# A two-layer trunk on one core: the first norm's squares in token layout, the gates' products in other banks, and a rebuilt start

## The chip, the cores and the metric

One core of a Trainium2 chip runs the whole program. Its engines are TensorE (PE: matmuls; PEld: the loads of their weights), VectorE (DVE), ScalarE (ACT), GpSimd (POOL) and SyncE (SP, which here only issues DMAs). Each works through its own instructions in order and waits on semaphores for the others. The metric is the device time of one execution in microseconds, the lower the better.

## The reference

The input x has 1024 tokens of 1024 numbers (fp32). Two layers follow, each a token mixer and a squared-ReLU MLP with residuals: the mixer of layer 0 is an mLSTM with 4 heads, that of layer 1 differential attention. A last norm ends it. The change lies in the first norm and in the mLSTM's input products and gates:

```python
def rmsnorm(x, g):
    y = xf * lax.rsqrt(jnp.mean(xf * xf, axis=-1, keepdims=True) + EPS)
    return (y * g.astype(jnp.float32)).astype(x.dtype)
...
    q, k, v, o, ig, fg = jnp.split(u @ w_in, splits, axis=-1)      # u = rmsnorm(h, ln_mix[0])
    log_i = softcap(ig.astype(f32) + bg[:nh], GATE_SOFTCAP)
    log_f = jax.nn.log_sigmoid(softcap(fg.astype(f32) + bg[nh:], GATE_SOFTCAP))
...
    b = jnp.cumsum(lf, axis=-1)                                    # inside each chunk of 128 tokens
    m_new = jnp.maximum(bl + m_st, ml)                             # from chunk to chunk, 8 chunks
...
    h = h + mix
    h = h + sq_relu_mlp(rmsnorm(h, ln_mlp[i]), w_up[i], w_down[i])
```

## The kernel before, in words

Activations are kept transposed: `h` has 128 channels on the partitions, 8 channel tiles `d`, and 1024 tokens along the free axis in two halves of 512. Products are made in three parts from split numbers (`hi` times `hi`, weight `lo` times `hi`, weight `hi` times `lo`), 128x512 each, so one panel of 128 output channels takes 2 halves x 8 tiles x 3 = 48 products (L1183 to L1185). The norm is applied after the product: a product leaves PSUM through `take` (L2465, VectorE), which multiplies it by `rstd_bc`, the reciprocal root of the mean square of each token, spread over all partitions.

The order on every engine is the order in which the code is written, apart from semaphores. The start, before:

- SyncE loads x in 8 pieces (`x_tok`, tokens on the partitions), then the gates' bias and `lam`, then panels of weights.
- For each of 8 channel tiles TensorE transposes 8 blocks of x into `aps` (L1446). VectorE copies the first half of the tokens to `h` (L2821), ScalarE the second (L2091). ScalarE rounds `h` times the norm's gain to `one_hi` (L2094), VectorE makes the rest, `one_lo` (L2406). ScalarE squares `h` (L2101), VectorE adds the squares of two tiles (L2816), and TensorE sums them over channels with 8 products by a column of ones (L1433, into `mps`), four times.
- The gate products (36 columns in two parts, L1462, L1463, L1466) follow their tile by two steps, into `dps`.
- `norm(0)` makes `rstd` on VectorE (L2442 and the chain behind it), TensorE spreads it (L1222, inside the first half of the first panel), VectorE copies it to `rstd_bc` (L2446).

Then come six panels, called panel 0 to 5 here. Each has two halves that take turns in the two `dps` banks; a half may start when the half before the last has been taken (`evac`). GpSimd splits the weights of a panel into hi and lo (L909, L914) and between two splits subtracts activation blocks (L1069) that ScalarE scales first (L2109) and rounds after (L2119). Beside the panels ScalarE and VectorE work out the gates: tanh, exp and log (L2146 to L2151), running sums (L2945), a running maximum over 8 chunks (L2955, L2959) with two subtractions for each chunk (L2962, L2968), exponentials (L2160 to L2164), then the selection of rows. TensorE joins in with 8 transposes (`gate_transposes`, L1478) and 4 products that spread one head's rows (`broadcast_rows`, L1487). VectorE reads these (`take_rows`, L2982, L2986) and splits the first weights of the next stage (`mix_low`, L2865). That stage, the mixer's products for the other heads (`mix_steps`, from L1506), starts behind panel 5. Its first product waits for the `take` of panel 5's first half and for `mix_low(0)`. Its first product is called the mix start here.

## Time and profile before

| | |
|---|---|
| three runs | 2242.74, 2242.92, 2241.22 us (median 2242.74) |
| profiled execution, first to last instruction | 2241.5 us (1.2 us under the median; what lies outside the span isn't listed by itself) |
| TensorE busy | 2209.4 us, 99% |
| TensorE weight loads | 1836.1 us, 82% |
| VectorE, ScalarE, GpSimd busy | 1640.5, 973.7, 873.3 us (73%, 43%, 39%) |
| first product of panel 0 | at 38.35 us |
| mix start | at 108.98 us |

A busy share is a mean over the whole span. Matmuls overlap, so a row of 390 ns with the next row 227 ns behind it stands for 227 ns of TensorE's time. The granted clock (PEclk) is a share of full speed.

### The profile page before, as it was taken

Reading aid. Unit: us, or ns where it says so; the run is one execution under the profiler, and the core shown is the slowest. Engines: PE = TensorE matmul, PEld = TensorE weight load, DVE = VectorE, ACT = ScalarE, POOL = GpSimd, SP = SyncE. Lnnn points to the kernel's source line nnn. Section 1 sums busy time; section 2 is a strip of 40 time slices with the busy share of each in tenths; the row PEclk is TensorE's granted clock in tenths of the full one; section 3 lists DMA queues with packets and bytes.
Section 4 is the critical chain, followed back from the end, with each engine's and each line's share of the span. In section 5 each row is a group of like instructions: output and inputs, shape, how many; then the busy total and the mean of one; then the engine's idle time right before and its main releaser. Section 6 shows DMA issues by size and latency. Waiting matters only on the chain.

```text
span 2241.5 us, 28700 instructions
## 1 busy us (share of the span) xinstructions
PE 2209.4 (99%) x10501; PEld 1836.1 (82%) x10501; DVE 1640.5 (73%) x2141; ACT 973.7 (43%) x1613; POOL 873.3 (39%) x805
## 2 busy tenths in 40 slices
PE   8999999999999999999999999999999999999998
PEld 6888887888888888888888888877888888888887
DVE  6867766499659479399577777786599569388397
ACT  6354444244343343345244455564354243343346
POOL 4845546200234233230766666675200234232320
PEclk9999999999999999999999999999999999999999
DMA  8677743363551632701522222222463542633601
GB/s 256 222 269 253 242 150 98 124 262 118 188 188 38 248 128 98 272 25 36 162 67 66 66 66 66 66 76 76 159 226 113 196 179 71 248 113 123 234 0 76
DMA packets 139844, 317.37 MB, mean 142 GB/s; under 512 B 8609, under 2 KB 82514, under 8 KB 126546
## 3 DMA queue, kind: packets, MB, share of 16 engines
q1 hardware_dynamic: 137552, 315.78, 41.1%
q8 instruction: 73, 1.20, 0.2%
q10 hardware_dynamic: 2178, 0.06, 0.1%
q14 instruction: 41, 0.34, 0.0%
HBM read 242.41 MB, written 56.62 MB: 133 GB/s over the span
## 4 chain that ended last, share of the span: by engine, by line
PE 92%; DVE 4%; ACT 2%; issue 1%; DMA 0%; POOL 0%; ACTq 0%; DVEq 0%; POOLq 0%
PE aps L1317 10%; PE aps L1321 10%; PE aps L1319 10%; PE mps L1317 4%; PE mps L1321 4%; PE dps L1317 4%; PE dps L1321 4%; PE mps L1319 4%; PE dps L1319 4%; PE dps L1183 3%; PE dps L1185 3%; PE dps L1184 3%; PE dps L1201 3%; PE dps L1203 3%; PE dps L1202 3%; PE mps L1677 2%
## 5 line engine op out<-in xcount | busy, mean ns | idle before, releaser
L1317 PE MATMUL aps<-b_ring,w_hi 128*128 128x512 f32 x640 | 249.3, 390 | 0.0
L1321 PE MATMUL aps<-b_ring,w_hi 128*128 128x512 f32 x640 | 249.0, 389 | 0.0
L1319 PE MATMUL aps<-b_ring,w_lo 128*128 128x512 f32 x640 | 249.0, 389 | 0.0
L1031 POOL TENSOR_TENSOR s_blk<-s_blk,a 128x1024 f32<-128x1024 f32 x24 | 68.6, 2859 | 379.4 <-DVE w_lo L2521 253.1
L2539 DVE TENSOR_TENSOR b_ring<-h,b_ring 128x1024 fp32r<-128x1024 f32 x120 | 206.3, 1726 | 5.6 <-ACT b_ring L1915 5.6
L909 POOL TENSOR_TENSOR w_hi<-w_raw,ones 128x256 fp32r<-128x256 f32 (+1 forms) x133 | 121.9, 946 | 201.7 <-PE dps L1203 103.8
L1023 POOL TENSOR_TENSOR s_blk<-a,a22u 128x1024 f32<-128x1024 f32 x12 | 34.9, 2907 | 327.0 <-DMA a<-in_w_up 320.0
L1317 PE MATMUL aps<-b_ring,a_hi 128*128 128x512 f32 x384 | 149.8, 390 | 0.0
L1321 PE MATMUL aps<-b_ring,a_hi 128*128 128x512 f32 x384 | 149.4, 389 | 0.0
L1319 PE MATMUL aps<-b_ring,a_lo 128*128 128x512 f32 x384 | 149.4, 389 | 0.0
L1317 PEld LDWEIGHTS aps<-b_ring,w_hi 128*128 128x128 f32 x640 | 120.1, 188 | 25.4 <-issue 0.7
L1319 PEld LDWEIGHTS aps<-b_ring,w_lo 128*128 128x128 f32 x640 | 120.1, 188 | 25.0
L1321 PEld LDWEIGHTS aps<-b_ring,w_hi 128*128 128x128 f32 x640 | 120.1, 188 | 25.0
L1915 ACT ACTIVATE b_ring<-h 128x1024 fp32r<-128x1024 f32 x112 | 116.5, 1048 | 49.8 <-DVE h L2574 35.1
L1201 PE MATMUL dps<-one_hi,w_hi 128*128 128x512 f32 x320 | 136.6, 427 | 0.0
L1879 ACT ACTIVATE w_hi<-s_blk 128x1024 fp32r<-128x1024 f32 x68 | 71.9, 1058 | 135.1 <-PE aps L1321 92.0
L1943 ACT ACTIVATE h<-h 128x1024 f32<-128x1024 f32 x64 | 67.8, 1060 | 140.6 <-DVE h L2643 132.3
L2521 DVE TENSOR_TENSOR w_lo<-s_blk,w_hi 128x1024 fp32r<-128x1024 f32 x68 | 87.7, 1289 | 53.3 <-ACT w_hi L1879 53.3
L1203 PE MATMUL dps<-one_lo,w_hi 128*128 128x512 f32 x320 | 126.0, 394 | 0.0
L1202 PE MATMUL dps<-one_hi,w_lo 128*128 128x512 f32 x320 | 125.5, 392 | 0.0
L2328 ACT ACTIVATE at<-mps 128x384 f32<-128x384 f32 (+2 forms) x120 | 46.9, 425 | 158.0 <-PE mps L1670 157.7
L914 POOL TENSOR_TENSOR w_lo<-w_raw,w_hi 128x256 fp32r<-128x256 f32 (+1 forms) x133 | 112.3, 873 | 2.9
(514 smaller groups left out, 6363.0 us busy)
## 6 DMA issues: line engine op xcount, KB each, us to landing
b_ring<-xs SPq DMA_DIRECT2D x42, 2048.0 KB, 7.9
xs<-b_ring SPq DMA_DIRECT2D x14, 2048.0 KB, 7.8
one_hi<-xm SPq DMA_DIRECT2D x19, 1024.0 KB, 5.0
one_lo<-xm SPq DMA_DIRECT2D x19, 1024.0 KB, 7.5
a<-in_w_up SPq DMA_DIRECT2D x16, 1024.0 KB, 5.4
a<-in_w_down SPq DMA_DIRECT2D x16, 1024.0 KB, 7.9
w_raw<-in_diff_w_in SPq DMA_DIRECT2D x24, 512.0 KB, 4.0
mix_a<-in_mlstm_w_in SPq DMA_DIRECT2D x36, 256.0 KB, 7.4
```

Of the source, the lines that this page charges most:

```text
L909: last = nc.gpsimd.tensor_tensor(hi[:, cut], w_raw[:, slot, cut], ones[:, :].unsqueeze(1).broadcast_to([P, piece, P]), ALU.mult)
L914: last = nc.gpsimd.tensor_tensor(lo[:, cut], w_raw[:, slot, cut], hi[:, cut].bitcast(f32), ALU.subtract)
L1201: nc.tensor.matmul(dps[:, half], w_hi[:, slot, k], rh, start=(k == 0), stop=False)
L1202: nc.tensor.matmul(dps[:, half], w_lo[:, slot, k], rh, start=False, stop=False)
L1203: last = nc.tensor.matmul(dps[:, half], w_hi[:, slot, k], rl, start=False, stop=(k == NT - 1))
L1317: nc.tensor.matmul(to[:, n], wh, ring[:, 0, k], start=new and k == 0, stop=False, skip_group_check=not new)
L1319: nc.tensor.matmul(to[:, n], wl, ring[:, 0, k], start=False, stop=False, skip_group_check=not new)
L1321: last = nc.tensor.matmul(to[:, n], wh, ring[:, 1, k], start=False, stop=(k == 3), skip_group_check=not new)
L1879: nc.scalar.activation(kt_view(A_HI[a % 3]), half_of(RAW[name], q), ACT.Copy).then_inc(a_hi, 1)
L1915: last = nc.scalar.activation(to, tiles_of(src, q), ACT.Copy)
L2521: nc.vector.tensor_tensor(kt_view(A_LO[a % 3]), half_of(RAW[name], q), kt_view(A_HI[a % 3]).bitcast(f32), ALU.subtract).then_inc(a_ready, 1)
L2539: last = nc.vector.tensor_tensor(lo, tiles_of(src, q), hi, ALU.subtract)
```

## The change

1. `sum_pair`, `add_squares` and the squares of `h` go: no squares in the loop over tiles. Behind the loop ScalarE squares `x_tok` in its own layout, 8 instructions of 128x1024 that also add up along the free axis (`accum_out`), which gives the sum of each token. `first_norm` makes `rstd` from it; it is spread after the first tile of panel 1.
2. The gate products go to `mps` and follow their tile by three steps; VectorE makes `one_lo` of tile 0 before it splits the gates' weights.
3. TensorE starts with 8 products of `ones` by `ones` into `dps`, which nothing reads.
4. Panel 0's high part is made by ScalarE behind tile 5; GpSimd makes only the low part.
5. Panel 0 goes to `dps`, panel 1 to `aps` banks 2 and 3, panel 2 to `dps`: the first two panels wait for no `take`. `gate_transposes` moves into panel 5 (it was in panel 4), and `broadcast_rows` from between panels 4 and 5 to behind panel 5.
6. On VectorE small constant work moves ahead of the norm; the 16 subtractions of the gates become two over all chunks. SyncE issues the bias and `lam` behind the first two panels' weights.

```diff
-            split(1, 1, 1, first=True, piece=PIECE)
+            low_part(1, 1, panel0_hi, 1)
@@ TensorE @@
-            def half_panel(g, slot, half, hi, lo, ready=None, base=0, hooks={}, order=range(NT), taken=None, weights=None):
+            def half_panel(g, slot, half, hi, lo, ready=None, base=0, hooks={}, order=range(NT), taken=None, weights=None,
+                           to=None):
+                to = dps[:, half] if to is None else to
...
-                pe.wait_ge(evac, 2 * g + half - 1 if taken is None else taken)
+                if taken != 0:
+                    pe.wait_ge(evac, 2 * g + half - 1 if taken is None else taken)
...
-            def sum_pair(p):
-                pe.wait_ge(sq_added, p + 1)
-                for j in range(NB):
-                    last = nc.tensor.matmul(mps[:, 0, j:j + 1], squares_of(2 * p)[:, j // 4, (j % 4) * P:(j % 4 + 1) * P],
-                                            ones[:, 0:1], start=first, stop=True, skip_group_check=not first)
...
+            pe.wait_ge(pool_chain, 4)
+            for n in range(8):
+                nc.tensor.matmul(dps[:, 0, 0:P], ones[:, :], ones[:, :], start=True, stop=True)
             pe.wait_ge(const_ok, 4)
-            for s in range(NT + 2):
+            for s in range(NT + GATE_LAG):
...
-                    if s % 2 == 1:
-                        sum_pair((s - 3) // 2)
-
-            half_panel(G_MIX[0], G_MIX[0] % 2, 0, *one, hooks={3: lambda: broadcast_rstd(0)})
-            half_panel(G_MIX[0], G_MIX[0] % 2, 1, *one)
+            g = G_MIX[0]
+            for half in range(2):
+                half_panel(g, g % 2, half, *one, taken=0)
+            for half in range(2):
+                half_panel(g + 1, (g + 1) % 2, half, *one, taken=0, to=aps[:, 2 + half],
+                           hooks={0: lambda: broadcast_rstd(0)} if half == 0 else {})
+            for half in range(2):
+                half_panel(g + 2, g % 2, half, *one, taken=3 + half)
...
-            panels(G_MIX[0], G_MIX[0] % 2, 4, *one, skip=1)
-            half_panel(G_MIX[0] + 4, (G_MIX[0] + 4) % 2, 0, *one)
+            panels(G_MIX[0], G_MIX[0] % 2, 5, *one, skip=3)
+            half_panel(G_MIX[0] + 5, (G_MIX[0] + 5) % 2, 0, *one)
             gate_transposes()
-            half_panel(G_MIX[0] + 4, (G_MIX[0] + 4) % 2, 1, *one)
+            half_panel(G_MIX[0] + 5, (G_MIX[0] + 5) % 2, 1, *one)
             pe.wait_ge(gates_ready, 1)
             broadcast_rows(0)
-            panels(G_MIX[0], G_MIX[0] % 2, 6, *one, skip=5)
@@ ScalarE, in the loop over tiles and behind it @@
-                for half in range(2):
-                    last = nc.scalar.activation(squares_of(d)[:, half], h[:, d, cuts[half]], ACT.Square)
-                last.then_inc(sq_ready, 1)
+                if d == 5:
+                    act.wait_ge(w_ld[1], 16)
+                    nc.scalar.activation(w_hi[:, 1], w_raw[:, 1], ACT.Copy).then_inc(panel0_hi, 1)
...
+            for n in range(NB):
+                last = nc.scalar.activation(x_tok[:, n], x_tok[:, n], ACT.Square, accum_out=small[:, 4, n:n + 1])
+            last.then_inc(ss_done, 1)
@@ VectorE @@
-            def add_squares(p):
-                dve.wait_ge(sq_ready, 2 * p + 2)
-                to = squares_of(2 * p)
-                nc.vector.tensor_tensor(to[:, :, :], to[:, :, :], sq[:, :, :], ALU.add).then_inc(sq_added, 1)
...
-            mlstm_takes(0, 0, 16)
+            mlstm_takes(0, 0, 32)
...
-            mlstm_takes(0, 16, 24)
+            mlstm_takes(0, 32, 40)
             for c in range(NB):
-                if c == 4:
-                    mlstm_takes(0, 32, 40)
...
-                if c == 5:
+                if c == 3:
                     mlstm_takes(0, 40, 48)
-                nc.vector.tensor_scalar(g_astate[:, chunk[c]], g_m[:, chunk[c]], mst[:, c:c + 1], None,
-                                        ALU.subtract)
...
+            nc.vector.tensor_tensor(by_chunk[0], by_chunk[1], mst[:, 0:NB].unsqueeze(2).broadcast_to([MH, NB, P]),
+                                    ALU.subtract)
+            nc.vector.tensor_tensor(by_chunk[2], by_chunk[3], by_chunk[1][:, :, P - 1:P].broadcast_to([MH, NB, P]),
+                                    ALU.subtract)
+            mlstm_takes(0, 48, 56)
```

`mlstm_takes(0, a, b)` takes the halves between a/8 and b/8: 0 and 1 are panel 0's, 2 and 3 panel 1's, and so on.

On VectorE a piece of the loop over tiles, before (the third and the fourth tile, with the add of squares between them):

```order
L2821 COPY h<-aps 128x512 [waits xt_done]
L2406 SCALAR_TENSOR_TENSOR one_lo<-h,gains,one_hi 128x512 [waits emit_hi] x2
L2816 TENSOR_TENSOR relu<-relu,sq 128x1024 [waits sq_ready]
L2821 COPY h<-aps 128x512 [waits xt_done]
L2406 SCALAR_TENSOR_TENSOR one_lo<-h,gains,one_hi 128x512 [waits emit_hi] x2
```

The same engine, now, from the second tile's copy on:

```order
L2822 COPY h<-aps 128x512 [waits xt_done]
L2407 SCALAR_TENSOR_TENSOR one_lo<-h,gains,one_hi 128x512 [waits emit_hi,gain_ready]
L2407 SCALAR_TENSOR_TENSOR one_lo<-h,gains,one_hi 128x512 [waits emit_hi]
L2834 CAST w_hi<-w_raw 128x8x64 [waits gate_ld]
L2835 TENSOR_TENSOR w_hi<-w_raw,w_hi 128x8x36 [waits dve_chain]
L2822 COPY h<-aps 128x512 [waits xt_done]
L2407 SCALAR_TENSOR_TENSOR one_lo<-h,gains,one_hi 128x512 [waits emit_hi] x2
L2822 COPY h<-aps 128x512 [waits xt_done]
```

The four adds of 128x1024 are gone, and the gates' weights are split one step later, behind tile 0's low part.

On TensorE the end of the panels, before (L1478 the gates' transposes, L1487 the spread rows, L1506 the mix start):

```order
L1478 MATMUL aps<-ident,mo 128x128 x7
L1183 MATMUL dps<-one_hi,w_hi 128x512 [waits evac]
...
L1487 MATMUL aps<-rows_hl,sel 128x512 [waits sel_ready,gates_ready]
L1487 MATMUL aps<-rows_hl,sel 128x512 x3
L1183 MATMUL dps<-one_hi,w_hi 128x512 [waits evac,w_split]
...
L1506 MATMUL dps<-one_hi,w_hi 128x512 [waits evac,mx_lo]
```

The same place now:

```order
L1478 MATMUL aps<-ident,mo 128x128 x7
L1184 MATMUL dps<-one_hi,w_hi 128x512 [waits evac]
...
L1487 MATMUL aps<-rows_hl,sel 128x512 [waits sel_ready,gates_ready]
L1487 MATMUL aps<-rows_hl,sel 128x512 x3
L1506 MATMUL dps<-one_hi,w_hi 128x512 [waits evac,mx_lo]
```

The panel that stood between the spread rows and the mix start has moved ahead of them. On VectorE the order around this place is as it was; the reader of the spread rows and the next stage's first splits, now:

```order
L2998 COPY cols<-aps 128x32 [waits gt_done]
L2998 COPY cols<-aps 128x32 x2
L3001 MEMSET small 128x1 [waits dve_chain]
L2472 SCALAR_TENSOR_TENSOR mo<-dps,rstd_bc 128x512 [waits half_done]
L2979 TENSOR_TENSOR nm<-aps,mask_sl 128x512 [waits rb_done]
L2979 TENSOR_TENSOR nm<-aps,mask_sl 128x512
L2983 COPY sq<-aps 128x512 x2
L2881 TENSOR_TENSOR w_lo<-mix_a,w_hi 128x512 [waits mx_hi] x2
L2472 SCALAR_TENSOR_TENSOR mo<-dps,rstd_bc 128x512 [waits half_done]
```

The two takes (L2472) are those of panel 4's second half and of panel 5's first half, as before.

## Rows read from the trace of the kernel before

**Rows 1.** The three stretches, busy us by engine (x instructions), PEclk, DMA share, GB/s.

```profile
0.00:38.35 38.35, 28.90 (x161) 22.98 (x162) 25.88 (x34) 27.52 (x45) 12.90 (x21) 0.96 0.79 223
38.35:108.98 70.63, 69.84 (x318) 57.25 (x318) 57.49 (x98) 24.15 (x25) 59.13 (x70) 1.00 0.73 244
108.98:2241.50 2132.52, 2110.67 (x10025) 1755.91 (x10023) 1557.12 (x2010) 922.06 (x1544) 801.23 (x716) 1.00 0.40 137
```

**Rows 2.** Timeline, loop over tiles: start us, us, engine, line.

```profile
12.26 0.46 DVE L2829 TENSOR_TENSOR w_hi<-w_raw,w_hi 128x288 fp32r<-128x288 f32 x1
12.63 1.41 DVE L2406 SCALAR_TENSOR_TENSOR one_lo<-h,gains,one_hi 128x512 fp32r<-128x512 f32 x2
...
17.99 1.33 ACT L2094 ACTIVATE one_hi<-h,gains 128x512 fp32r<-128x512 f32 x2
...
25.57 2.43 DVE L2406 SCALAR_TENSOR_TENSOR one_lo<-h,gains,one_hi 128x512 fp32r<-128x512 f32 x2
...
26.40 4.03 POOL L914 TENSOR_TENSOR w_lo<-w_raw,w_hi 128x256 fp32r<-128x256 f32 x4
...
36.55 1.95 PE L1433 MATMUL mps<-ones,acc 128*128 128x1 f32 x16 [0.49 <-DVE acc L2816]
```

**Rows 3.** The same columns as rows 1, three stretches inside the loop.

```profile
24.00:25.00 1.00, 0.09 (x1) 0.00 (x0) 1.00 (x2) 0.44 (x1) 1.00 (x1) 1.00 0.95 410
25.00:30.00 5.00, 4.89 (x29) 4.12 (x30) 4.59 (x7) 3.83 (x7) 4.92 (x6) 0.74 0.43 180
30.00:35.00 5.00, 5.00 (x34) 4.13 (x33) 5.00 (x7) 4.29 (x8) 0.43 (x1) 0.91 0.00 0
```

**Rows 4.** Timeline of TensorE: first panel product, the wait in panel 2, mix start.

```profile
38.35 0.48 PE L1183 MATMUL dps<-one_hi,w_hi 128*128 128x512 f32 x1
...
63.23 0.47 PE L1183 MATMUL dps<-one_hi,w_hi 128*128 128x512 f32 x1 [0.56 <-DVE m_in L2465]
...
108.98 0.39 PE L1506 MATMUL dps<-one_hi,w_hi 128*128 128x512 f32 x1
```

**Rows 5.** Timeline, gates: ScalarE's first and scaling, VectorE's scans, an accumulator read.

```profile
47.27 1.15 ACT L2146 ACTIVATE sq<-relu,gbias 4x1024 f32<-4x1024 f32 x1 [7.54 <-DVE gbias L2926]
...
55.56 4.26 ACT L2109 ACTIVATE h<-h,gains 128x1024 f32<-128x1024 f32 x4
...
124.01 0.20 ACT L2213 ACTIVATION_READ_ACCUMULATOR relu<-aps 128x1 f32 x1
```

**Rows 6.** Timeline of VectorE: running sums, their add, one chunk's maximum and carry.

```profile
54.17 6.58 DVE L2945 TENSOR_TENSOR_SCAN hn<-nm 4x128 f32<-4x128 f32 x8 [1.65 <-ACT hn L2151]
60.78 1.58 DVE L2950 TENSOR_TENSOR mo<-hn 4x1024 f32<-4x1024 f32 x1
...
69.54 0.87 DVE L2955 TENSOR_TENSOR_SCAN mo<-mo,mst 4x128 f32<-4x128 f32 x1
70.45 0.51 DVE L2959 TENSOR_TENSOR mst<-mo,hn 4x1 f32<-4x1 f32 x1
```

**Rows 7.** Timeline of GpSimd: a subtraction block and one panel's split.

```profile
57.98 3.30 POOL L1069 TENSOR_TENSOR h<-h 128x256 f32<-128x256 f32 x4
62.82 2.92 POOL L909 TENSOR_TENSOR w_hi<-w_raw,ones 128x256 fp32r<-128x256 f32 x4 [1.53 <-PE dps L1185]
65.81 2.94 POOL L914 TENSOR_TENSOR w_lo<-w_raw,w_hi 128x256 fp32r<-128x256 f32 x4
```

**Rows 8.** Timeline of VectorE around the spread rows.

```profile
96.44 0.37 DVE L3001 COPY cols<-aps 128x32 f32<-128x32 f32 x3
...
98.26 1.29 DVE L2982 TENSOR_TENSOR nm<-aps,mask_sl 128x512 f32<-128x512 f32 x2 [0.23 <-PE aps L1487]
99.46 1.28 DVE L2986 COPY sq<-aps 128x512 f32<-128x512 f32 x2
100.66 2.45 DVE L2865 TENSOR_TENSOR w_lo<-mix_a,w_hi 128x512 fp32r<-128x512 f32 x2
103.74 0.69 DVE L2465 SCALAR_TENSOR_TENSOR mo<-dps,rstd_bc 128x512 f32<-128x512 f32 x1 [0.63 <-PE dps L1185]
```

More of the change, by code:

```diff
@@ L31 @@
 NB = S // P
+GATE_LAG = 3
 DFF = 4 * D
@@ L363, in h_block @@
             return h[:, t:t + 2, half * HALF:(half + 1) * HALF]
-        def squares_of(d):
-            return sq if d % 2 == 1 else (relu if d % 4 == 0 else acc)
         def flat(t):
@@ L654, in first_inputs @@
                 panel(1)
+                for j in range(2):
+                    sp.dma_start(gbias[32 * j:32 * j + MH, 0:1],
+                                 m_b[0, MH * j:MH * (j + 1)].rearrange("(p t) -> p t", t=1)).then_inc(const_ld, 16)
+                sp.dma_start(lam[:, :, :], a_lam[0].partition_broadcast(P)).then_inc(const_ld, 16)
                 sp.wait_ge(xt_copied, 4)
@@ L1182, in half_panel @@
                     rh, rl = piece(hi, k, half), piece(lo, k, half)
-                    nc.tensor.matmul(dps[:, half], wh[:, k], rh, start=(n == 0), stop=False)
-                    nc.tensor.matmul(dps[:, half], wl[:, k], rh, start=False, stop=False)
-                    last = nc.tensor.matmul(dps[:, half], wh[:, k], rl, start=False,
+                    nc.tensor.matmul(to, wh[:, k], rh, start=(n == 0), stop=False)
+                    nc.tensor.matmul(to, wl[:, k], rh, start=False, stop=False)
+                    last = nc.tensor.matmul(to, wh[:, k], rl, start=False,
                                             stop=(n == NT - 1))
@@ L2443, in norm, with first_norm @@
                 rsqrt_of_twice(v, rstd[:, :], t).then_inc(rstd_ready, 1)
-                if e == 0:
-                    dve.wait_ge(bc_done, 1)
-                    nc.vector.tensor_copy(rstd_bc[:, 0], aps[:, 0])
-                    ch.link(nc.vector.tensor_copy(rstd_bc[:, 1], aps[:, 1]))
+            def first_norm():
+                dve.wait_ge(ss_done, 1)
+                v, t = small[:, 5], small[:, 6]
+                ch.link(nc.vector.tensor_scalar(v, small[:, 4], 0.5 / D, 0.5 * EPS, ALU.mult, ALU.add))
+                rsqrt_of_twice(v, rstd[:, :], t).then_inc(rstd_ready, 1)
+                dve.wait_ge(bc_done, 1)
+                nc.vector.tensor_copy(rstd_bc[:, 0], aps[:, 0])
+                ch.link(nc.vector.tensor_copy(rstd_bc[:, 1], aps[:, 1]))
             def norm_half(e, half, sums):
@@ L2460, in copy_rstd, with take @@
                 ch.link(nc.vector.tensor_copy(rstd_bc[:, half], aps[:, half]))
-            def take(g, half, dst, scale=1.0):
+            def take(g, half, dst, scale=1.0, bank=None):
                 dve.wait_ge(half_done, 2 * g + half + 1)
-                nc.vector.scalar_tensor_tensor(dst, dps[:, half], scale, rstd_bc[:, half], ALU.mult,
+                nc.vector.scalar_tensor_tensor(dst, dps[:, half] if bank is None else bank, scale, rstd_bc[:, half], ALU.mult,
                                                ALU.mult).then_inc(evac, 1)
@@ L2825, in _ @@
                 if s == 1:
+                    dve.wait_ge(gain_ready, 1)
+                if s >= 1:
+                    for half in range(2):
+                        emit(0, s - 1, half, 2 * (s - 1) + half)
+                if s == 1:
                     used = slice(0, 32 + MH)
@@ L2830, in _ @@
                                             w_hi[:, 0, :, used].bitcast(f32), ALU.subtract).then_inc(gate_split, 1)
-                    dve.wait_ge(gain_ready, 1)
-                if s >= 1:
-                    for half in range(2):
-                        emit(0, s - 1, half, 2 * (s - 1) + half)
-                if s >= 2 and s % 2 == 0:
-                    add_squares(s // 2 - 1)
             for half in range(2):
@@ L2852, in mlstm_takes @@
                         dst, half = dsts[u // 16], (u // 8) % 2
-                        take(G_MIX[0] + u // 16, half, dst[:, half * HALF:(half + 1) * HALF])
+                        take(G_MIX[0] + u // 16, half, dst[:, half * HALF:(half + 1) * HALF],
+                             bank=aps[:, 2 + half] if u // 16 == 1 else None)
             def low_of_t(t, q):
```

69 lines of the change are left out of this document (29 added, 40 removed).

## The prediction, made before the changed kernel was run

> **What bounds the kernel now.** I read the stretches first. Behind the mix start TensorE is busy for 2110.67 of 2132.52 us, and nothing there is edited [rows 1]. Between panel 0 and the mix start it is busy for 69.84 of 70.63 us, so 0.79 us idle is all that is to be had there. Before panel 0 lie 38.35 us, in which TensorE counts as busy for 28.90 but works for others: the timeline of the loop over tiles shows VectorE with two low parts in 1.41 us, a copy out of PSUM at the 0.69 us that such a read takes, and the adds of squares, and behind it a last sum of squares of 1.95 us on TensorE [rows 2, 8]. So the start is bound by VectorE's work per tile, the rest of the stretch by TensorE, and what the change can win is the distance by which panel 0 comes earlier. The question is whether everything that TensorE needs between panel 0 and the mix start comes earlier too. For that I read the gates, GpSimd's splits and the place around the spread rows [rows 5 to 8].
>
> **Panel 0 starts earlier: -9.9 us.** The split of the gates' weights waits for its DMA and ends at 12.72 us [rows 2]; in the changed order it lies behind tile 0's low part, and x arrives as before. From there VectorE has six rounds of one copy (0.69) and two low parts (1.41), 2.10 us each: 12.7 + 12.6 = 25.3. The last tile's low part adds 1.4. GpSimd now runs the low part of panel 0's weights (4.03 us) in the last two rounds, and a pair of low parts beside it took 2.43 instead of 1.41 us, so 1.0 more. Two last gate products, 0.39 us each and partly overlapped [rows 4], add 0.7. Panel 0 starts at 28.4 instead of 38.35 us. ScalarE keeps up: two roundings 1.33 us and a copy of about 0.6 are under 2.10, and its one copy of panel 0's weights costs 1.07 (4.26 / 4) [rows 5] before the last two tiles, nearly covered. The bounds: 27.3 if the GpSimd collision costs nothing, 29.5 if TensorE at half clock paces a tile (8 transposes and 4 products). So -11.0 to -8.9. The eight constant products run before x has landed; I give them nothing, and a gain of 0.6 if they leave the clock up for the first tiles.
>
> **The idle time in the stretch goes: -0.8 us.** That is the wait of 0.56 us at 63.23 and the smaller one at the norm [rows 4], since the first two panels wait for no take. TensorE's busy work of the stretch is otherwise the same: twelve halves of 24 products at 227 ns are 65.4 us, with the transposes and spread products beside them.
>
> **GpSimd is late for panel 3: +2.4 us.** This is what is late next. The squares leave the loop, but ScalarE must do them before anything else: 8 of 128x1024 at 1.07 us and an accumulator read of 0.20 partly overlapped [rows 5], 9.6 us, from 26.3 to 35.9. The root of twelve tiny VectorE steps (some 2.4 us) is ready at 38.3; TensorE asks for it at 28.4 + 10.9 + 0.7 = 40.0, so no wait, 1.7 us to spare. Spreading, copying and scaling the gates takes 5.4 us, as before, and tanh starts at 45.4 instead of 47.27. From there ScalarE's chain is unchanged: the scaling of the upper tiles starts 8.3 us later (55.56 - 47.27), at 53.7. GpSimd needs two of these scalings (2.1), then its subtraction block (3.3), then panel 3's split (5.9) [rows 7]: 65.1 us. TensorE gets there at 28.4 + 6 x 5.45 + 1.8 = 62.9. It waits 2.2 us. Put plainly: panels come 10 us earlier, the gates and scalings only 2, and the slack in between was about 6. VectorE's own chain ends level with that: running sums 5 (6.58 before, some beside an idle GpSimd) from 52.6, add 1.6, eight chunks of 1.45 (0.87 and 0.51 with gaps) [rows 6], two wide subtractions of about 1.6 in place of sixteen small ones, and takes of 0.7 in between reach the take that panel 4 needs at 75.9; TensorE wants it at 76.0. By the exponentials, row parts and selection (11.4 us in all) the take for panel 5 is done at 87.3 against 86.9 wanted: 0.2 to 0.4 more. So +2.4, between 0 and 5.
>
> **Inside panel 5: +1.5 us.** Its second half waits for the take of panel 4's second half, and on VectorE that take stands behind the column copies, which wait for the gates' transposes that TensorE has only just finished. In a row: copies and link 0.6, take 0.7, semaphores 0.2 [rows 8]. Before, the half behind the transposes waited for a take that stood ahead of them. 1.3 to 1.8.
>
> **Between the spread rows and the mix start: +5.1 us.** Before, 10.9 us of panel 5 lay here. Now the mix start stands right behind the spread rows, and on VectorE its two conditions stand behind the reading of these rows: two adds and two copies (98.26 to 100.66, 2.4 us), two weight splits (2.45, or 1.41 for two of that size where GpSimd is quiet), and the take of panel 5's first half, 0.7 [rows 2, 8]. That is 4.5 to 5.6 us; I take 5.1. Queued behind the waiting product is the whole next stage.
>
> **The clock after that wait: +1.7 us.** In the loop over tiles TensorE was busy 0.09 of 1 us and then with single-column sums; after this the granted clock was 0.74 over 5 us and 0.91 over the next 5 [rows 3]: 5 x 0.26 + 5 x 0.09 = 1.75 us of TensorE's work lost, at the level of 1.2 GHz for the stretch in which it was down. The new idle spell is longer than any in the old trace behind the loop, and dense products follow, so I charge 1.7; the bounds are 0 and 1.8. The Trainium skill ("TensorE: Matmul & The Clock Gate", "HAM oscillation — how this bites in real kernels") speaks against the change here: an idle gap inside a kernel puts the array back to half rate, and what follows starts cold. The trace agrees that it happens; with that rule the term is 1.7, without it 0.
>
> **The sum.** -9.9 - 0.8 + 2.4 + 1.5 + 5.1 + 1.7 = 0.0 us. The span stays at 2241.5, and the time at the median of 2242.74, 1.2 above the span: 2242.7. All low ends together give -11.0 - 0.8 + 0 + 1.3 + 4.5 + 0 = -6.0, all high ends -8.9 - 0.8 + 5 + 1.8 + 5.6 + 1.8 = +4.5.
>
> **Rivals.** What a measurement of this kernel can tell from no change is about 0.2%, 4.5 us.
>
> *Most of the head start survives.* GpSimd is on time and the clock stays up: a start at 27.5 (-10.8), -0.8, 0.5 for the late parts, 1.5, 4.8: -4.8 us, 2237.9. For it: VectorE and GpSimd slow each other, and every figure of theirs that I use was taken with both busy (the pair of low parts at 2.43 against 1.41); if they overlap less, both chains shrink. Against it: both must shrink, since they end within half a microsecond of each other, and the two new waits of 1.5 and 4.5 or more don't depend on them. The Trainium skill ("GPSIMD Engine Reference", "1. Specifications") has the two engines share their SBUF interfaces where a VectorE instruction has two SBUF inputs; the low parts are such instructions, and the trace agrees.
>
> *The squares come too late (slower).* Place: the spread of the root behind the first tile of panel 1. No row shows a 1024-wide square with a sum; only the read of the accumulator after a narrow one. With 1.7 us to spare it decides from 9.6 + 1.7 = 11.3 us for eight, 1.4 us each. At 2.0 us each (twice a plain pass) the root comes 16.0 - 11.3 = 4.7 us late, TensorE waits that long, and as gates, scalings and GpSimd hang on the same root, all behind it moves by as much: +4.7, and with a second clock loss of about 1: +5.7, 2248.4. Against it: wide ScalarE passes in this trace are 1.06 to 1.15 us whatever the function.
>
> *The change does not do what it says.* The constant products may leave the clock where it was when the first tile comes. The transposes of the first tiles then cost as before, which is what my sum assumes. It decides 0.6 us.
>
> **How the numbers follow.** No change 0.67, within -4.5 and +4.5; its own range is 2239.5 to 2245.5. The head start survives and more than 4.5 us are left 0.21. Slower by over 4.5 us 0.12: the late squares, or GpSimd's lateness at its upper bound. The range with 8 chances in 10 is 2237.6 to 2246.4: into the faster case, and just short of the slower.
>
> **What would show it.** In the changed profile: panel 0 near 28.4 us; eight squares near 1.2 us each and no wait at the spread root; a wait of about 2 us on GpSimd's w_lo at panel 3, one of 1.5 us on a VectorE take inside panel 5, one of about 5 us on a VectorE take at the first product of the next stage, and a granted clock under 1 behind it; the mix start near 107.3 instead of 108.98, with the clock loss following it. I am wrong if the mix start comes before 104, if the wait ahead of it is under 3 us, if panel 0 starts after 31, or if new waits appear behind the mix start.

## The result, and the profile after

The changed kernel takes 2247.36 us (median of 13 runs, 2245.44 to 2248.07), the kernel before on the same chip 2242.81 (13 runs, 2241.17 to 2244.50): a ratio of 1.0018, 95% interval 1.0011 to 1.0024, so slower by 2.5 to 5.4 us. The forecast was 2242.7 with a range up to 2246.4. The result lies 1 us above the range.

The stretches of the changed kernel, in the columns of [rows 1]; the third is the first chunk of the mixer's products, from the mix start to the transposes behind them:

```profile
0.00:28.06 28.06, 21.16 (x114) 16.05 (x114) 18.64 (x28) 19.43 (x32) 6.40 (x16) 0.94 1.00 268
28.06:109.20 81.14, 70.53 (x317) 56.98 (x316) 54.76 (x86) 35.37 (x42) 69.16 (x81) 0.99 0.69 234
109.20:120.25 11.05, 11.05 (x37) 8.80 (x37) 8.42 (x10) 3.17 (x3) 8.82 (x10) 0.73 0.26 96
120.25:2245.80 2125.55, 2102.61 (x9989) 1749.39 (x9987) 1546.41 (x2001) 916.18 (x1538) 784.15 (x695) 1.00 0.39 136
```

The kernel before, with the same cuts behind its mix start:

```profile
108.98:117.15 8.17, 8.17 (x38) 6.71 (x37) 7.00 (x9) 5.51 (x6) 7.87 (x9) 1.00 0.61 213
117.15:2241.50 2124.35, 2102.50 (x9989) 1749.20 (x9987) 1550.13 (x2001) 916.55 (x1538) 793.36 (x708) 1.00 0.40 136
```

Panel 0 starts 10.3 us earlier (28.06 against 38.35) and the mix start is 0.2 us later (109.20 against 108.98). All of the head start is lost between the two: the second stretch is 10.5 us longer than before, with 10.6 us idle on TensorE instead of 0.8. The third is 2.9 us longer for as many products, and the rest 1.2. The sum is -10.3 + 10.5 + 2.9 + 1.2 = +4.3, which is the difference of the spans (2245.8 - 2241.5).

What TensorE waited for between 25 and 125 us (released by; us in total, times, longest), changed kernel:

```profile
PE dps L1506 <- DVE mo L2472: 5.0, 1, 5.0
PE dps L1184 <- POOL w_lo L911: 4.3, 3, 2.5
PE mps L1458 <- DVE one_lo L2407: 1.5, 3, 0.5
PE dps L1184 <- DVE mo L2472: 1.2, 1, 1.2
```

The first row is the mix start, the second panels 3, 4 and 5, the fourth the second half of panel 5. Together 10.5 us; the third lies in the loop over tiles. The timeline of TensorE at panel 3 and at the mix start, to be held against [rows 4]:

```profile
62.62 0.39 PE L1186 MATMUL dps<-one_lo,w_hi 128*128 128x512 f32 x1
65.51 0.50 PE L1184 MATMUL dps<-one_hi,w_hi 128*128 128x512 f32 x1 [2.50 <-POOL w_lo L911]
65.85 0.39 PE L1185 MATMUL dps<-one_hi,w_lo 128*128 128x512 f32 x1
...
109.20 0.77 PE L1506 MATMUL dps<-one_hi,w_hi 128*128 128x512 f32 x1 [5.01 <-DVE mo L2472]
109.77 0.63 PE L1507 MATMUL dps<-one_hi,w_lo 128*128 128x512 f32 x1
...
114.89 0.48 PE L1507 MATMUL dps<-one_hi,w_lo 128*128 128x512 f32 x1
115.21 0.40 PE L1508 MATMUL dps<-one_lo,w_hi 128*128 128x512 f32 x1
```

A wait costs a little more than its idle time. The product ahead of it counts with all of its 0.39 us instead of the 0.227 to the next start, and behind the first product 0.34 us pass instead of 0.227: 0.28 us more of busy time for each wait.

From 109.20 to 114.89 stand 13 products at 0.43 us from start to start where 0.23 is the rule: that is the level of 1.2 GHz, and 13 x 0.2 = 2.6 of the 2.9 us. The granted clock says the same (windows, columns as above):

```profile
105.00:109.00 4.00, 0.00 (x0) 0.00 (x0) 4.00 (x7) 0.75 (x1) 3.92 (x5) 0.91 0.00 0
109.00:110.00 1.00, 0.80 (x2) 0.73 (x3) 1.00 (x2) 0.00 (x0) 0.92 (x2) 0.50 0.00 0
110.00:115.00 5.00, 5.00 (x13) 3.84 (x13) 3.31 (x5) 2.21 (x2) 3.79 (x5) 0.50 0.49 183
```

GpSimd behind the scalings, the rows that answer to [rows 7]:

```profile
56.17 3.28 POOL L1066 TENSOR_TENSOR h<-h 128x256 f32<-128x256 f32 x4 [7.88 <-ACT h L2110]
59.42 3.06 POOL L906 TENSOR_TENSOR w_hi<-w_raw,ones 128x256 fp32r<-128x256 f32 x4
62.57 2.89 POOL L911 TENSOR_TENSOR w_lo<-w_raw,w_hi 128x256 fp32r<-128x256 f32 x4
...
71.59 5.64 POOL L911 TENSOR_TENSOR w_lo<-w_raw,w_hi 128x256 fp32r<-128x256 f32 x4
77.19 4.84 POOL L1066 TENSOR_TENSOR h<-h 128x256 f32<-128x256 f32 x4
82.00 4.78 POOL L906 TENSOR_TENSOR w_hi<-w_raw,ones 128x256 fp32r<-128x256 f32 x4
```

The blocks of 4.8 to 5.6 us are not new. In the kernel before two of the same work stand at 85.67 us, beside VectorE's third wide subtraction, its low parts of 128x1024 and its row parts (84.98 to 94.54); TensorE did not wait for them:

```profile
85.67 5.24 POOL L909 TENSOR_TENSOR w_hi<-w_raw,ones 128x256 fp32r<-128x256 f32 x4 [2.04 <-PE dps L1185]
90.98 4.84 POOL L914 TENSOR_TENSOR w_lo<-w_raw,w_hi 128x256 fp32r<-128x256 f32 x4
```

VectorE in the changed kernel beside GpSimd's slow blocks, and around the spread rows ([rows 6, 8] before):

```profile
70.86 1.73 DVE L2962 TENSOR_TENSOR nm<-mo,mst 4x1024 f32<-4x1024 f32 x1
72.61 1.67 DVE L2964 TENSOR_TENSOR nm<-mo 4x1024 f32<-4x1024 f32 x1
...
104.23 1.29 DVE L2979 TENSOR_TENSOR nm<-aps,mask_sl 128x512 f32<-128x512 f32 x2 [6.76 <-PE aps L1487]
105.43 1.28 DVE L2983 COPY sq<-aps 128x512 f32<-128x512 f32 x2
106.63 1.83 DVE L2881 TENSOR_TENSOR w_lo<-mix_a,w_hi 128x512 fp32r<-128x512 f32 x2
108.38 0.68 DVE L2472 SCALAR_TENSOR_TENSOR mo<-dps,rstd_bc 128x512 f32<-128x512 f32 x1
```

The line at 104.23 is one to look at twice: VectorE had been idle for 6.76 us when the spread rows came. The take of panel 5's first half, on which the mix start hangs, could have been made in that time; it stands behind the rows only in the order of the code.

### The profile page after: what moved, and what is told of

Its sections match the earlier page's. It is cut to its first block, busy times and chain, and to the rows that moved or that the text cites. A ratio compares the mean times of both kernels' runs of the same rounds, so it can differ in the third digit from the quotient of the medians.

```text
span 2245.8 us, 28587 instructions
## 1 busy us (share of the span) xinstructions
PE 2205.3 (98%) x10453; PEld 1831.2 (82%) x10453; DVE 1628.2 (73%) x2123; ACT 974.2 (43%) x1614; POOL 868.5 (39%) x801
## 4 chain that ended last, share of the span: by engine, by line
PE 89%; DVE 3%; ACT 1%; issue 1%; DMA 0%; ACTq 0%; SPq 0%; DVEq 0%
PE aps L1318 10%; PE aps L1320 10%; PE aps L1322 10%; PE mps L1318 4%; PE dps L1318 4%; PE mps L1322 4%; PE mps L1320 4%; PE dps L1322 4%; PE dps L1320 4%; PE dps L1202 3%; PE dps L1204 3%; PE dps L1203 3%; PE dps L1184 3%; PE dps L1185 3%; PE dps L1186 3%; PE mps L1676 2%
## 5 line engine op out<-in xcount | busy, mean ns | idle before, releaser
L906 POOL TENSOR_TENSOR w_hi<-w_raw,ones 128x256 fp32r<-128x256 f32 (+1 forms) x129 | 117.3, 939 | 168.4 <-PE dps L1204 104.0
L1318 PE MATMUL dps<-b_ring,w_hi 128*128 128x512 f32 x288 | 112.3, 390 | 0.0
```

The source lines that it names most:

```text
L906: last = nc.gpsimd.tensor_tensor(hi[:, cut], w_raw[:, slot, cut], ones[:, :].unsqueeze(1).broadcast_to([P, piece, P]), ALU.mult)
L1318: nc.tensor.matmul(to[:, n], wh, ring[:, 0, k], start=new and k == 0, stop=False, skip_group_check=not new)
```

## The experiments

Each was timed beside the kernel before on the same chip, and ratios are to that kernel. The theory for all of them: the new start is worth what it seems, the new place of the gates' transposes and spread rows costs more than that, and GpSimd's lateness and a fall of the clock take the rest. The rival: the start itself does not carry through, and any place gives no gain.

**The old place with the new start.** The gates' transposes go back into panel 4, the spread rows back between panels 4 and 5; all else is the changed kernel.

```diff
-            panels(G_MIX[0], G_MIX[0] % 2, 5, *one, skip=3)
-            half_panel(G_MIX[0] + 5, (G_MIX[0] + 5) % 2, 0, *one)
+            panels(G_MIX[0], G_MIX[0] % 2, 4, *one, skip=3)
+            half_panel(G_MIX[0] + 4, (G_MIX[0] + 4) % 2, 0, *one)
             gate_transposes()
...
             broadcast_rows(0)
+            panels(G_MIX[0], G_MIX[0] % 2, 6, *one, skip=5)
```

> Changed kernel with one part undone: the gates' transposes are back inside panel 4, the spread rows back between panels 4 and 5. Theory (this move alone turned the gain into a loss, because panel 5 no longer covers the reading of the rows and the weight splits): gates ready by 88 us, rows spread near 90, panel 5 from 90 to 101, mix start near 101.2 at full clock; 2247.4 - 8.0 - 2.6 = 2236.8 us. Rival (the gates are too late for the old place, which is why they were moved): TensorE waits several us ahead of the spread rows, mix start at 104 or later, 2240 us or more.

Measured: 2237.20 us, ratio 0.9975 (0.9966 to 0.9984), mix start at 101.99. No wait is left at the mix start or inside panel 5. The one at panel 3 stays, and here the clock fell with it:

```profile
66.03 0.80 PE L1184 MATMUL dps<-one_hi,w_hi 128*128 128x512 f32 x1 [2.53 <-POOL w_lo L911]
66.62 0.63 PE L1185 MATMUL dps<-one_hi,w_lo 128*128 128x512 f32 x1
...
68.75 0.47 PE L1184 MATMUL dps<-one_hi,w_hi 128*128 128x512 f32 x1
```

Without the new place the change is a gain of 5.6 us (interval 3.6 to 7.6). The rival falls.

**The new place alone**, in the kernel before (the edit above the other way round).

> The kernel before with one part of the change alone: the gates' transposes in panel 5 and the spread rows behind panel 5. Theory (the new place costs a wait of 1.2 to 1.5 us inside panel 5, one of 5.0 us at the mix start and the low clock of some 2.6 us behind it, whatever the start does): mix start at 115 to 116 instead of 109, granted clock 0.5 to 0.85 from there for 5 us, and 2250.5 to 2252.5 us, so 8 to 9 us above before. Rival (the waits of the new place come from the gates being 8 us earlier than the panels in the changed kernel, not from the place): 2244 to 2247 us.

Measured: 2253.05 us, ratio 1.0046 (1.0033 to 1.0060), so +10.3 with an interval of 7.4 to 13.5. The waits of its trace, from 36 to 118 us, are those of the changed kernel without GpSimd's, and one more of 0.6 us on a take in panel 4:

```profile
PE dps L1506 <- DVE mo L2464: 5.0, 1, 5.0
PE dps L1183 <- DVE mo L2464: 1.8, 2, 1.2
```

The mix start is at 114.15 us, 5.2 later than before. In this execution panel 0 started at 36.78, though nothing ahead of it was edited; from there the mix start is 77.37 us away instead of 70.63. Seven products at the low clock follow (1.4 us). The theory held on the waits; the time lies half a microsecond above its band. The profiled execution (2249.93) is the fastest of the five and 7.2 us above the profiled one of the kernel before; the other 3 of the 10.3 us stand in no trace. The three slowest of the five show a mean granted clock of 0.994 to 0.995 against 0.998 in the profiled one, so the low clock lasted longer there; where, is not shown. The two parts of the change measured apart give -5.6 + 10.3 = +4.7, and the whole +4.0, which is agreement within these intervals and no more.

**The spread rows read later.** On VectorE the next stage's first two splits and both takes of panel 5 move ahead of the reading of the spread rows.

```diff
             mlstm_takes(0, 4 * 16 + 8, 5 * 16)
-            take_rows(0)
             mix_low(0)
             mix_low(1)
             mlstm_takes(0, 10 * 8, 11 * 8)
-            low_of_t(T2, 0)
             mlstm_takes(0, 11 * 8, 6 * 16)
+            take_rows(0)
             mix_low(2)
+            low_of_t(T2, 0)
```

> Changed kernel with one edit on VectorE: the reading of the spread rows moves behind the first two weight splits and the takes of panel 5, which are all that the mix start waits for. Theory (the wait of 5.0 us ahead of the mix start is VectorE's order, and the clock falls because of it): the wait is under 0.5 us, the clock stays at 1.00 behind it, the mix start comes at 104.3 instead of 109.2 us and no product runs at 0.63 us; 2247.4 - 4.9 - 2.6 = 2239.9 us. Rival (the time of that wait is given back at the next one, since the rows are read later and the chunks need them): a wait before the first chunk's transposes takes 2 to 3 us, and the time stays over 2243.

Measured: 2240.37 us, ratio 0.9989 (0.9980 to 0.9998). The mix start follows the spread rows at once, at full clock, and the 4.3 us for GpSimd and 1.2 us in panel 5 stay:

```profile
102.78 1.10 PE L1487 MATMUL aps<-rows_hl,sel 128*128 128x512 f32 x4
103.72 0.39 PE L1506 MATMUL dps<-one_hi,w_hi 128*128 128x512 f32 x1
```

Some seven of the lost microseconds (2247.4 - 2240.4; 6.5 by the ratios) hang on where VectorE reads the spread rows: 5.0 of wait and the rest clock.

**The clock by itself.** 16 products of ones by ones, which nothing reads, fill the wait behind the spread rows.

```diff
             broadcast_rows(0)
+            for n in range(16):
+                nc.tensor.matmul(mps[:, 1, 0:P], ones[:, :], ones[:, :], start=True, stop=True)
```

> Changed kernel with 16 more products of ones by ones on TensorE, 4.1 us, put into the wait of 5.0 us ahead of the mix start; nothing reads them. Theory (the idle spell is what brings the clock down, and the half-speed stretch behind it costs some 2.6 us): mix start stays at 109.2, granted clock 1.00 behind it, the products there 0.39 instead of 0.63 us; 2247.4 - 2.6 = 2244.8 us. Rival (the fallen clock costs nothing, since VectorE's chain paces the next stage anyway): granted clock 1.00, but a new wait takes the gain and the time stays at 2247.4.

Measured: 2244.44 us, ratio 1.0005 (0.9996 to 1.0014). The wait shows as 1.5 us, the rest of it is filled, and the products behind it take 0.40 us:

```profile
105.19 3.73 PE L1573 MATMUL mps<-ones 128*128 128x128 f32 x32
110.39 0.47 PE L1506 MATMUL dps<-one_hi,w_hi 128*128 128x512 f32 x1 [1.48 <-DVE mo L2474]
```

The wait is no shorter, only busy, and the time falls by 2.9 us. That is the size of the clock's share, but not a clean measure of it: this profile also lacks a wait of 1.4 us behind the first chunk that the changed kernel's has, and the two intervals together leave 2 to 3 us either way. (The mix start came 1.2 us later than in the changed kernel's profile; in this execution the first panel products ran at the low clock.)

**GpSimd on time.** ScalarE scales the upper four tiles ahead of the gates' tanh instead of behind their exponential.

```diff
-            for d in range(4):
+            for d in range(NT):
                 scale_x(d)
...
-            for d in range(4, NT):
-                scale_x(d)
```

> Changed kernel with one edit on ScalarE: the scaling of tiles 4 to 7 goes ahead of the gates' tanh, into the 7.4 us in which ScalarE waits. Theory (GpSimd is late for panels 3 to 5 because its subtraction blocks wait for these scalings): the waits for w_lo (2.5, 0.6 and 1.25 us) go, but VectorE's gate chain then binds panel 5, whose first half starts near 87.6 instead of 89.7; about -2, 2245.3 us, with the 5 us wait and the fallen clock still there. Rival (GpSimd alone binds, VectorE's chain has slack): panel 5 starts near 84.5, -5, 2242.3 us.

Measured: 2246.49 us, ratio 1.0013 (1.0004 to 1.0022). All three waits on GpSimd are gone (4.3 us), and 2.8 us on a VectorE take in panel 4 stand in their place. The gates' tanh began 0.7 us later (46.33), but that is the smaller part. VectorE's eight running sums of 4x128 took 6.21 us, with GpSimd splitting weights beside them from 53.5 us on; in the changed kernel they ran while GpSimd stood idle, in 2.61. The clock took the rest: TensorE is idle for 8.7 us of the stretch instead of 10.6, but busy for 72.4 instead of 70.5, because seven products behind the new wait (77.91) and the first ones of panel 0 ran at 0.63 us. The mix start comes at 109.31, as late as without the edit.

**The same with the old place**, and one take ahead of a wait for ScalarE's exponentials.

> The changed kernel with the gates' transposes and the spread rows in their old places (2237.2 us was measured for that alone), with all eight scalings of the activations on ScalarE ahead of the gates' tanh, and with VectorE's take of panel 4's first half ahead of its wait for ScalarE's exponentials. Theory (GpSimd's wait of 2.5 us at panel 3 and the low clock of 2.7 us behind it are what the old place still loses, some 3.5 us, and the gates' chain on VectorE, 2.1 us later, has the slack for it): no wait over 0.7 us between panel 0 and the mix start, mix start at 98.5 to 100, 2233.5 to 2235 us. Rival (the gates' chain takes the place of GpSimd, as it did when only the scalings were moved: 2.8 us at a take in panel 4): a wait of 2 us or more on a VectorE take at panel 4 or on gates_ready, mix start at 101 to 103, 2236.5 to 2238.5 us.

Measured: 2236.61 us, ratio 0.9961 (0.9947 to 0.9976), mix start at 101.27. The rival was right on the mechanism: 2.8 us at a VectorE take in panel 4, mix start between 101 and 103. VectorE's rows show why that take was late:

```profile
73.29 1.22 DVE L2961 TENSOR_TENSOR nm<-mo,mst 4x1024 f32<-4x1024 f32 x1
74.53 1.74 DVE L2963 TENSOR_TENSOR nm<-mo 4x1024 f32<-4x1024 f32 x1
76.28 0.69 DVE L2471 SCALAR_TENSOR_TENSOR m_in<-dps,rstd_bc 128x512 f32<-128x512 f32 x1
```

It stands behind the two wide subtractions, which panel 4 does not need.

**The old place and the late reading together.**

> The changed kernel with the gates' transposes and spread rows in their old places and, on VectorE, the next stage's first two weight splits and both takes of panel 5 ahead of the reading of the spread rows. Theory (with the old place there is no wait left at the mix start that the order on VectorE could remove): mix start at 101.5 to 102.5 as in the old place alone, 2236.7 to 2237.8 us. Rival A (the two edits each win about 7 to 10 us and add up): 2232 us or less. Rival B (the takes of panel 5 now stand ahead of the reading, which the first head's next product needs, and that wait is new): 2239 us or more.

Measured: 2237.92 us, ratio 0.9970 (0.9959 to 0.9980), mix start at 101.80 without a wait, and one of 0.7 us for a weight split 9.5 us behind it. As the theory said: two cures for one wait do not add up.

**Subtractions by chunk.** The two wide subtractions become 16 small ones in the loop over chunks again.

```diff
+                nc.vector.tensor_scalar(g_astate[:, chunk[c]], g_m[:, chunk[c]], mst[:, c:c + 1], None, ALU.subtract)
+                nc.vector.tensor_scalar(g_akey[:, chunk[c]], g_g[:, chunk[c]], g_m[:, end], None, ALU.subtract)
-            nc.vector.tensor_tensor(by_chunk[0], by_chunk[1], mst[:, 0:NB].unsqueeze(2).broadcast_to([MH, NB, P]),
-                                    ALU.subtract)
-            nc.vector.tensor_tensor(by_chunk[2], by_chunk[3], by_chunk[1][:, :, P - 1:P].broadcast_to([MH, NB, P]),
-                                    ALU.subtract)
```

> The changed kernel with the gates' two subtractions over all chunks (1024 wide, at 70.9 to 74.3 us, beside GpSimd's slowest block: four low parts in 5.64 instead of about 3 us) made chunk by chunk again, 16 instructions inside the loop over chunks. Theory (the wide subtractions are what slows GpSimd in that stretch and make it late for panels 4 and 5 by 0.6 and 1.3 us): GpSimd's block at 71.6 takes 3 to 4 us, the waits on w_lo at panels 4 and 5 fall under 1 us together, and the time is 2246 to 2247.2 us. Rival A (the sixteen small subtractions, about 0.5 us each beside a busy GpSimd, cost VectorE 4 us more than the wide ones and its takes come late): a wait of 2 us or more on a take at panel 4, 2248.5 us or more. Rival B (neither sets the waits): within 0.5 us of 2247.4 with the same waits.

Measured: 2251.57 us, ratio 1.0034 (1.0021 to 1.0048). GpSimd's blocks, the same work as in the changed kernel:

```profile
71.91 2.83 POOL L911 TENSOR_TENSOR w_lo<-w_raw,w_hi 128x256 fp32r<-128x256 f32 x4
74.70 2.94 POOL L1066 TENSOR_TENSOR h<-h 128x256 f32<-128x256 f32 x4
79.14 2.77 POOL L906 TENSOR_TENSOR w_hi<-w_raw,ones 128x256 fp32r<-128x256 f32 x4 [1.50 <-PE dps L1186]
81.98 5.81 POOL L911 TENSOR_TENSOR w_lo<-w_raw,w_hi 128x256 fp32r<-128x256 f32 x4
```

```profile
82.15 0.47 PE L1184 MATMUL dps<-one_hi,w_hi 128*128 128x512 f32 x1 [3.16 <-DVE m_in L2472]
```

The theory's time is missed by 4 us, rival A's is met; on the mechanism both are true at once. Beside the small subtractions GpSimd's block takes 2.83 us instead of 5.64, and its waits at panels 4 and 5 are gone; and rival A's price is paid: VectorE's chain through the chunks is 7 us longer (the take behind it starts at 81.31 instead of 74.28) and TensorE waits 3.2 us for it. But the slow block has only moved: at 81.98, when VectorE comes to its third wide subtraction (82.03) and the low parts, GpSimd takes 5.81 us. So the edit does not show that the two subtractions alone made GpSimd late; it shows that a block is slow where VectorE's wide work stands beside it. The idle time of the stretch grew by only 1.2 us. The larger part of the loss is the clock's: 8 products behind each of the waits at panels 3 and 4 ran at 0.63 us, which behind panel 3's did not happen in the changed kernel, and TensorE was busy for 74.0 us instead of 70.5. That the wide subtractions are a gain in sum holds with this in it.

**The eight constant products**, taken out of the changed kernel, and put alone into the kernel before.

```diff
-            pe.wait_ge(pool_chain, 4)
-            for n in range(8):
-                nc.tensor.matmul(dps[:, 0, 0:P], ones[:, :], ones[:, :], start=True, stop=True)
```

> The changed kernel without the eight constant products that TensorE runs while x is loaded. In the changed profile the first eight transposes take 1.04 us, before 1.94. Theory (they lift the clock for the first tiles, but VectorE's 2.1 us per tile sets the start, so little of it arrives): the first transposes cost 1.9 us again, panel 0 starts 0 to 0.7 us later than 28.06, and the time is 2247.4 to 2248.1 us. Rival A (TensorE paces the first tiles, and its fall to half clock between 12.3 and 16.6 us comes from the idle after a busy start): without them the start is the same or earlier, 2246.5 to 2247.4. Rival B (the start hangs on them): panel 0 after 29.5, 2249 us or more.

> The kernel before with nothing but the eight constant products ahead of the first transposes. Theory: the first transposes take 1.0 instead of 1.9 us, but the loop over tiles waits for VectorE, and panel 0 starts at 37.7 to 38.4 us; the time is 2242.2 to 2243.0, no difference to before. Rival (the clock in the loop over tiles is worth more than one tile): panel 0 before 37.5 us and a time under 2242.0.

Measured: without them 2247.10 us, ratio 1.0013 (1.0004 to 1.0022); alone 2244.91, ratio 1.0003 (0.9993 to 1.0012). The first tile's transposes, changed kernel, and the same without the products:

```profile
5.87 1.04 PE L1441 MATMUL aps<-ident,x_tok 128*128 128x128 f32 x8
```

```profile
5.37 1.94 PE L1438 MATMUL aps<-ident,x_tok 128*128 128x128 f32 x8 [5.37 <-DMA x_tok<-in_x]
```

In the changed kernel's profile they lift the clock of the first tile, as was meant. That is not sure: in the other versions that have them these eight take between 1.04 and 1.91 us. The second tile's take 1.06 to 1.24 us with them and 1.97 without. Panel 0 starts at 27.97 us without them and at 28.06 with them, and the time is that of rival A, the same within the noise. Rival A's reason is not settled: the fall of the clock between 12 and 17 us of the changed kernel's profile (0.66) is missing here, but also in three versions that have the products (filled wait, old place, same with early scalings). In the loop VectorE sets the pace. With them alone in the kernel before panel 0 came at 36.15 us in the profiled execution, which the rival had asked for; the time shows nothing of it, and the untouched start of the new place alone gave 36.78 against 38.35. So this start varies by more than a microsecond from one execution to the next.

**Every take ahead of what it does not need.** The new places, the early scalings, the late reading of the rows, and each take of panels 3 and 4 ahead of the gates' work that it stood behind.

```diff
+            mlstm_takes(0, 48, 56)
             by_chunk = [t.rearrange("p (c l) -> p c l", l=P) for t in (g_astate, g_m, g_akey, g_g)]
...
+            mlstm_takes(0, 7 * 8, 4 * 16)
             low_of_t(T1, 0)
-            mlstm_takes(0, 7 * 8, 4 * 16)
             low_of_t(T1, 1)
+            mlstm_takes(0, 4 * 16, 4 * 16 + 8)
             dve.wait_ge(gate_act, 3)
...
+            mlstm_takes(0, 4 * 16 + 8, 5 * 16)
             dve.wait_ge(gt_done, 1)
```

> The changed kernel with its new places kept, the eight scalings ahead of the gates' tanh, the takes of panel 3's and panel 4's halves each moved ahead of VectorE's gate work that they stood behind (the two wide subtractions, a low part, the wait for the exponentials, the column copies), and the next stage's first two splits with both takes of panel 5 ahead of the reading of the spread rows. Theory (every idle microsecond between panel 0 and the mix start comes from the order on VectorE and ScalarE, none from their work as such): no wait over 0.7 us in the stretch, mix start at 97.9 to 99, full clock, 2231 to 2233.5 us. Rival (the gates' chain itself is the bound: transposes and rows can't be ready earlier): a wait of 1.5 us or more at the gates' transposes or the spread rows, 2235 us or more.

Measured: 2234.03 us, ratio 0.9958 (0.9944 to 0.9971). That is 9.4 us under the kernel before, against which it was timed, and some 13 under the changed one. Half a microsecond above the expected band. TensorE is never idle between panel 0 and the mix start:

```profile
28.17:98.29 70.12, 70.12 (x317) 58.15 (x316) 56.99 (x81) 33.50 (x41) 62.09 (x69) 0.98 0.72 243
98.29:2232.20 2133.91, 2112.12 (x10025) 1757.43 (x10023) 1558.97 (x2014) 921.57 (x1543) 804.11 (x717) 1.00 0.40 137
```

This is the fastest version measured. The gates' chain was no bound; the places in the order were. The wait of 5.0 us, the 1.2 in panel 5 and GpSimd's 4.3 are all gone with moved instructions alone, though GpSimd still has slow blocks (5.44 and 4.68 us): with the scalings early it is ahead of the panels when they come.

## Why the prediction was wrong

The places where TensorE would wait, and for whom, were right. Two terms of the sum were too small, GpSimd's by 1.9 us and the clock's by 1.2, and two costs were put at nothing: the busy time that each wait adds (0.7) and the stretch behind the first chunk (1.2). All four err in the same direction.

**Panel 0, -9.9.** Measured -10.3 (28.06; forecast 28.4). The squares took 1.04 us from start to start with the accumulator read inside (forecast 1.2), and nothing waited for the root in the changed kernel. That was luck: of the 1.7 us to spare nothing was left. The root's last steps ran beside GpSimd at 0.66 us each instead of 0.17, it was ready at 39.78 us, and TensorE spread it at 39.83. In three other versions TensorE waited 0.5 to 0.6 us for it.

```profile
39.11 0.67 DVE L2427 SCALAR_TENSOR_TENSOR rstd<-small,rstd 128x8 f32<-128x8 f32 x1
39.83 2.05 PE L1223 MATMUL aps<-ident,rstd 128*128 128x128 f32 x16
```

The reference point was softer than I took it: 38.35 is one execution's number, and an unedited start gave 36.78 in another.

**Idle in the stretch, -0.8.** As forecast: neither of the two old waits is left.

**GpSimd late for panel 3, +2.4.** This term was mis-sized: measured 4.3. At panel 3 it was right (2.50 us, forecast 2.2; GpSimd done at 65.5, forecast 65.1). What I put at 0.2 to 0.4 behind that were 0.6 and 1.2 us at panels 4 and 5, again for GpSimd. I had charged its next blocks at the durations of [rows 7], 2.9 to 3.3 us. They took 5.64, 4.84 and 4.78. The step that failed is this price: [rows 7] shows GpSimd beside VectorE's running sums and small chunk work only, and the same trace had the other price, 5.24 and 4.84 us at 85.67, beside the third wide subtraction, the low parts of 128x1024 and the row parts. In the changed kernel the two new wide subtractions stand beside the first slow block, and I priced them for VectorE alone (1.6 each; measured 1.73 and 1.67); beside the other two stands work that was there before. It cost nothing there because GpSimd was ahead of the panels. The subtractions by chunk bear it out: three blocks at 2.83, 2.94 and 2.77 us, and the next, beside the third wide subtraction, at 5.81. The Trainium skill ("GPSIMD Engine Reference", "1. Specifications"), which the prediction weighed only as a reason why things might go better, has the two engines share their SBUF interfaces under VectorE instructions with two SBUF inputs; the trace agrees, for GpSimd as for VectorE.

**Inside panel 5, +1.5.** Measured 1.2, by the wait named. The new place alone gave the same 1.2.

**Between the spread rows and the mix start, +5.1.** Measured 5.0, on the take named. The late reading and the new place alone each confirm it.

**The clock, +1.7.** The second mis-sized term, and beyond its bound of 1.8: 2.9 us behind the mix start by the windows, 2.6 by counting products. I took the loss from [rows 3], where the clock stood at 0.74 and 0.91 over two stretches of 5 us, as the most that a spell can cost. Those two shares stand for 3.5 us at the low level; here it lasted 5.7 us, all of it filled with products.

**The busy time of waits, 0.** The stretch from panel 0 to the mix start has 0.7 us of busy time more than before, and the sum had no term for it. The changed kernel has five waits there, the kernel before two; three more at 0.28 us each, as read above at panel 3, are 0.8, a little less because the product behind the last wait lies outside the stretch.

**Behind the first chunk, 0.** Measured +1.2. TensorE waits 1.4 us more for the DMA of `q_lo` before the attention's products. Of the other profiled executions seven have a good part of that wait (among them the late reading, the early scalings and the subtractions by chunk), three have none of it (the filled wait, the new place alone, the last version), one has 0.4 us (the constant products alone); no edit separates them. I take it for scatter between executions, but it isn't settled.

The sum by these measured terms: -10.3 - 0.8 + 4.3 + 1.2 + 5.0 + 0.7 + 2.9 + 1.2 = +4.2, the span's difference up to rounding; +0.0 was forecast. Of the miss 1.9 us are GpSimd's, 1.2 the clock's, 0.7 the busy time of the waits and 1.2 the tail's, less 0.8 where the change did better than forecast. The -10.3 carries the scatter of the start, so that the sum closes this well is in part luck.

**The rivals.** The surviving head start asked for both chains to shrink, and the one on VectorE did: its scans ran in 2.61 us. It did not help, since GpSimd was the later one. The late squares did not happen. That the constant products do nothing for the time is right, though not for the reason given: they can raise the clock of the first tile, and nobody waits for it. The range ended too low: all the high ends together came to +4.5 us, which is about what was measured, and I had cut them at +3.7. GpSimd's and the clock's high ends were not independent mishaps but followed from VectorE's wide instructions and from the change's own wait.

## What to carry to other kernels

When a phase is pulled forward, look at every instruction that stands ahead of a buffer's release on its engine and is not needed for it: here moving takes, splits and scalings past gate work and row reading was worth 13 us, three times what the whole change had lost. In this kernel VectorE's wide two-input instructions had two prices, one on VectorE and one for what GpSimd did beside them; take a block's duration from the row beside which it will stand. A new wait of 4.5 to 5.0 us in front of dense products cost the wait and then the clock, in all five versions that had it.

## What the runs showed of the hardware

- VectorE's eight running sums of 4x128 took 2.61 us with GpSimd idle and 6.21 with it busy, 0.33 against 0.78 us each. The width on the partitions (4 of 128) did not spare them.
- GpSimd's four instructions of 128x256 took 2.8 us beside VectorE's small chunk work, and 4.8 to 5.8 beside its subtractions of 4x1024 and 128x1024, in the kernel before as well (5.24, 4.84).
- A wait of 2.4 to 2.5 us at panel 3 stands in seven profiles. Behind it the clock stayed up in four (next product 0.39 us: the changed kernel, the late reading, the filled wait, the old place with the late reading) and fell in three (6 to 8 products at 0.63 us or more: the old place, without the constant products, the subtractions by chunk). The wait of 2.8 us at panel 4 went both ways too. Behind the waits of 4.5 to 5.0 us at the mix start it fell in all five, for 7 or 13 products. So the clock's fall is not a fixed price of a wait.
- Within the loop over tiles the clock fell at other times from kernel to kernel: panel 0's first product took 0.39 or 0.40 us in four of the versions with the new start and 0.63 in six, at a start of 27.8 to 28.3 us in all of them.
